# Ten wide matmuls on constants between the sums of squares and unit 0, and ten narrow ones fewer at the start

## What is computed

```python
def rmsnorm(x, g):
    y = x * lax.rsqrt(jnp.mean(x * x, axis=-1, keepdims=True) + EPS)
    return y * g

def ada_norm(x, g, shift, scale):
    return rmsnorm(x, g) * (1 + scale) + shift

for l in range(DEPTH):
    mod = (c @ w_ada[l] + b_ada[l]).reshape(B, N_SUB, 3, D_MODEL)[:, :, :, None, :]
    h = ada_norm(x, norm_gain[l, 0], mod[:, 0, 0], mod[:, 0, 1])
    x = x + 0.5 * mod[:, 0, 2] * swiglu(h, w_ffn_in[l, 0], w_ffn_out[l, 0])
    ...                     # the mixer with mod[:, 1], then the second feed-forward with mod[:, 2]
```

## Time and profile before

| | |
|---|---|
| Median of 3 runs | 1437.67 us (1437.45 to 1437.7) |
| The profiled execution's own time | 1436.94 us |
| Its span, first to last instruction | 1435.1 us |
| TensorE matmuls | 1420.1 us busy, 99% of the span |
| Chain that ended last | PE 91%, DVE 4%, issue 2%, ACT 1%, DMA 1% |
| Granted TensorE clock, mean | 0.998 |

### The profile page before, as it was taken

One profiled execution on the slowest core, in us unless ns is written; L12 is line 12 of the kernel. 1 busy time (PEld: TensorE's weight loads), 2 busy tenths in 40 slices (PEclk: granted clock), 3 DMA queues, 4 the chain that ended last, 5 costly groups with the idle time before them and its releaser, 6 DMA issues.

```text
span 1435.1 us, 33152 instructions
## 1 busy us (share of the span) xinstructions
PE 1420.1 (99%) x13908; PEld 1361.8 (95%) x13908; DVE 949.5 (66%) x1651; ACT 812.1 (57%) x1350; POOL 98.9 (7%) x154
## 2 busy tenths in 40 slices
PE   8999999999999999999999999999999999999998
PEld 6999999999999999999999999999999999999998
DVE  5664547779876697555575545587898677955553
ACT  3554435877676476344464444468876755744543
POOL 3030000001110210000000000000011002000000
PEclk9999999999999999999999999999999999999999
DMA  9988897689984669787768897676999557785661
GB/s 341 308 269 271 243 267 206 177 247 274 245 228 133 198 187 293 217 248 243 202 202 266 273 282 251 198 207 192 261 251 269 165 155 217 225 240 159 178 187 51
DMA packets 460414, 323.75 MB, mean 226 GB/s; under 512 B 11668, under 2 KB 436069, under 8 KB 460266
## 3 DMA queue, kind: packets, MB, share of 16 engines
q1 hardware_dynamic: 452240, 299.96, 71.0%
q0 software_dynamic: 7584, 20.51, 5.2%
q10 hardware_dynamic: 442, 1.17, 0.2%
HBM read 313.29 MB, written 8.37 MB: 224 GB/s over the span
## 4 chain that ended last, share of the span: by engine, by line
PE 91%; DVE 4%; issue 2%; ACT 1%; DMA 1%; ACTq 0%; DVEq 0%
PE bank L513 28%; PE bank L514 27%; PE bank L515 27%; PE bank L704 4%; DVE wlo L478 1%; PE bank L919 1%; DMA stage<-in_x_prompt 1%; PE bank L947 1%; PE bank L966 1%; DVE x L1973 0%; PE bank L988 0%; PE bank L923 0%; PE bank L742 0%; PE bank L1009 0%; ACT xA L1301 0%
## 5 line engine op out<-in xcount | busy, mean ns | idle before, releaser
L478 DVE TENSOR_TENSOR wlo<-raw,whi 128x1024 fp32r<-128x1024 f32 (+1 forms) x432 | 513.1, 1202 | 325.1 <-ACT whi L470 323.8
L513 PE MATMUL bank<-hH,whi 128*128 128x264 f32 x2016 | 578.1, 287 | 0.0
L514 PE MATMUL bank<-hL,whi 128*128 128x264 f32 x2016 | 571.7, 284 | 0.0
L515 PE MATMUL bank<-hH,wlo 128*128 128x264 f32 x2016 | 571.2, 283 | 0.0
L470 ACT ACTIVATE whi<-raw 128x1024 fp32r<-128x1024 f32 (+1 forms) x432 | 438.1, 1033 | 173.5 <-PE bank L515 168.9
L513 PEld LDWEIGHTS bank<-hH,whi 128*128 128x128 f32 x2016 | 379.7, 188 | 13.4 <-issue 12.8
L514 PEld LDWEIGHTS bank<-hL,whi 128*128 128x128 f32 x2016 | 380.0, 189 | 0.0
L515 PEld LDWEIGHTS bank<-hH,wlo 128*128 128x128 f32 x2016 | 378.2, 188 | 0.0
L513 PE MATMUL bank<-hidH,whi 128*128 128x264 f32 x704 | 200.7, 285 | 0.0
L515 PE MATMUL bank<-hidH,wlo 128*128 128x264 f32 x704 | 200.2, 284 | 0.0
L514 PE MATMUL bank<-hidL,whi 128*128 128x264 f32 x704 | 199.6, 284 | 0.0
(11 more groups left out here) (368 smaller groups left out, 1719.4 us busy)
## 6 DMA issues: line engine op xcount, KB each, us to landing
raw<-in_w_ffn_in SPq DMA_DIRECT2D x172, 512.0 KB, 4.8
raw<-in_w_in SPq DMA_DIRECT2D x120, 512.0 KB, 5.3
ring<-in_w_ada SPq DMA_DIRECT2D x96, 512.0 KB, 6.8
raw<-in_w_ffn_out SPq DMA_DIRECT2D x64, 512.0 KB, 4.8
raw<-in_w_ada SPq DMA_DIRECT2D x32, 512.0 KB, 4.1
raw<-in_w_ffn_out SPq DMA_DIRECT2D x32, 384.0 KB, 4.9
raw<-in_w_out SPq DMA_DIRECT2D x16, 512.0 KB, 5.0
out<-st POOLq DMA_DIRECT2D x12, 512.0 KB, 7.7
```

The lines of the kernel that those rows point to most:

```text
L478: nc.vector.tensor_tensor(wlo[:, s, 0:w], raw_unit(n)[:, 0:w], whi[:, s, 0:w].bitcast(F), ALU.subtract).then_inc(lo_done, 1)
L513: nc.tensor.matmul(out, a, rh, start=start, stop=False)
L514: nc.tensor.matmul(out, a, rl, start=False, stop=False)
L515: return nc.tensor.matmul(out, b, rh, start=False, stop=stop)
```

## The change

FILL goes from 43 to 33, and a new constant KEEP is 10. Between the last of the sums of squares and the first feed-forward, ten matmuls are issued on TensorE. Each multiplies 32 columns of the ones tile with its 256 columns, in fp32, into partitions 0 to 31 of the bank AUX[1]. They carry no wait and no semaphore update.

```diff
-FILL = 43
+FILL, KEEP = 33, 10
...
             ada_units(7, 1)
             for k in range(4, KT):
                 add_squares(k)
+            for _ in range(KEEP):
+                mm(AUX[1][0:32, 0:T], ones[:, 0:32], ones[:, :], start=True, stop=True)
             for L in range(NL):
                 ffn(L, 0)
                 mixer(L)
```

## The result

| | before | after |
|---|---|---|
| Median, 22 executions each | 1437.74 us | 1439.61 us |
| Lowest to highest | 1435.60 to 1439.62 | 1437.65 to 1440.89 |
| Ratio, 95% interval | | 1.0012 (1.0006 to 1.0017) |
| Profiled execution, its span | 1436.94, 1435.1 us | 1437.84, 1436.0 us |

The change costs 1.9 us in the median, with an interval of 0.9 to 2.4: slower, but within the 0.2% that the prediction took for no change. The profiled executions differ by 0.9 us.

The account below looks back on a forecast made before the run. TensorE bounds the kernel, with no slack behind the setup. Profiled execution 1436.94 + 0.99 (2.46 us of fillers on the path, unit 0 3.16 instead of 4.63) = 1437.9; against the median, 1438.7 us, range 1436.4 to 1441.8.

Parts of the forecast that it names:

- What bounds the kernel: TensorE, idle only 15.0 of 1435.1 us: whatever moves unit 0 of the first feed-forward moves the end by as much.
- Part 1 costs nothing: Ten small fillers fewer at the start: gain nothing, since line 713 waits for the stage transfer at 12.73 anyway; taken as 0.
- a sign of being wrong: The prediction counted itself wrong if line 713 moved from 12.7 us, fillers started side by side, or the clock fell before 40.
- The price of a wide filler: Between sums of squares and unit 0: twenty records of 0.218 us, 4.36 us; the gap hides 1.9, 2.46 go on the path.
- Does the clock stay high: Wide fillers in the gap before unit 0 hold the clock through 23 to 27 us; chance 0.63, at +0.9 to +1.6 us.
- The first rival: Wide fillers before unit 0 don't hold the clock, or lose it later: +2.6 or +4.4 to +6 us; chance 0.20.
- the rival of overlap: Wide fillers on one column group overlap each other and end inside the gap before unit 0: -1.3 us; chance 0.09.
- small fillers don't lift the clock: Argument against a held clock: start fillers on 32 of 128 columns kept TensorE busy at 4 to 8 us without lifting it.
- What comes back: With the clock held high, unit 0 takes 3.16 us instead of 4.63, ending at 28.61 against 27.62: net +0.99 us.
- The rival that the low stretch comes whatever TensorE does: The clock stays low at 23.1 to 26.5 us regardless, so the fillers run half in it: +2.6 us; chance 0.04.

Follow-up runs that it names:

- part 1 alone: 33 small fillers at the start and no wide ones, against the kernel before: 1445.2 us against 1437.01, ratio 1.0060 (1.0047 to 1.0073).
- 43 + 10: All 43 small fillers kept and ten wide ones added, against the kernel before: 1440.25 us against 1437.01, ratio 1.0020 (1.0011 to 1.0029).
- 38 + 5: 38 small fillers at the start and five wide ones in the gap, against the kernel before: 1436.32 us against 1437.44, ratio 0.9998 (0.9990 to 1.0007).
- 39 + 4: 39 small fillers at the start and four wide ones in the gap, against the kernel before: 1438.09 us against 1437.09, ratio 1.0008 (0.9999 to 1.0016).
- the kernels with the long start: 20 or 21 small and 15 96-column start fillers, three wide behind two modulation units, five or four in the gap, against before: 1435.98 or 1436.03 us.
- five wide: 33 small fillers at the start and five wide ones in the gap, against the kernel before: 1442.47 us, ratio 1.0033 (1.0021 to 1.0046).
- twenty wide: 33 small fillers at the start and twenty wide ones in the gap, against the kernel before: 1443.54 us, ratio 1.0041 (1.0027 to 1.0055).
- 23 + 20: 23 small fillers at the start and twenty wide ones in the gap, against the kernel before: 1444.09 us against 1437.44, ratio 1.0045 (1.0032 to 1.0059).

## Why the prediction was right, and what it mis-sized

**The forecast**, 1438.7 us and no measurable change, holds; the time lies in the range, and the profiled executions differ by 0.9 us where 0.99 was worked out. That this is so close is luck: the end of unit 0 moved by 0.6 and not by 0.99, and 0.2 us of a wait elsewhere and 0.1 unaccounted made up the rest. The median moved by 1.9.

**What bounds the kernel.** Right. What the fillers put in front of unit 0 reached the end: 0.6 us at line 704 behind it, 0.2 us in one wait, and 0.1 us unaccounted.

**Part 1 costs nothing.** Right for the reason given, the wait for the stage tile, and borne out with ten small fillers back in the program (ratio 0.9998, 0.9990 to 1.0007). Line 713 did move, to 12.33, which the prediction had as a sign of being wrong; but it moved with the tile's landing, which puts it anywhere from 12.3 to 13.3 in the traces with the short start, with no order by the number of fillers. The zero is right only because the number of matmuls stayed 43, which the prediction didn't see. Had the change dropped the ten without adding ten, it would have cost the 8 us of part 1 alone, outside the range. No row of before hinted at a size; the wait named issue near its end is 0.5 us.

**The price of a wide filler.** 0.218 us a record predicted, 0.216 measured, in two kernels. The gap hid 1.9 us of it and unit 0 starts 2.06 us later than before; 2.46 was worked out, and 0.3 of the 0.4 between them is that the fillers start at 20.64 and not at 20.93: the stage tile had landed 0.4 us earlier.

**Does the clock stay high.** Yes, through 4.4 us after, and through 8.8 us with twenty. The first rival, fillers that don't hold it, is out. So is the rival of overlap, by the 0.216. But one argument of the step was wrong: that small fillers don't lift the clock. They didn't in the execution that was read. They did in the profiled ones with 43 + 10, 38 + 5 and several others, by 7 to 9 us. The prediction read one execution of a thing that varies from one to the next; 1.07 against 1.93 us for the first two units of line 704 is the sign to look for.

**What comes back, the term that was mis-sized.** 1.47 us in unit 0, counted for every execution. It comes back only where the clock had fallen at 23 us. Of the kernels with nothing wide in the gap, the profiled executions of part 1 alone and of ten small ones in the gap have no fall there (unit 0 is over at 26.59 and 26.76); that with the ten moved behind the first mixer has it (28.41, from a start at 23.78). Counted from the end of the sums, unit 0 is over 6.5 and 6.7 us later where the clock falls (before, and the ten moved), 5.3 and 5.4 where it doesn't, and 7.4 in all three traces with ten wide fillers. So the fillers cost 0.7 to 0.9 us where the clock would have fallen, and 2.0 to 2.1 where it wouldn't. A mixture of these fits the 1.9 of the median, but it is argued, not shown: how many executions of before are of which kind can't be counted from their mean clocks. The view prints 0.998 for the execution before, with the fall at 23, for 39 + 4, whose fall is at 12, and for the kernels with the long start, which have none before the end. Nor does it say why both groups moved by at least 1.5.

**The rival that the low stretch comes whatever TensorE does.** Its price was 2.6 us; the profiled execution after has no fall at 23 us, and the ten executions at 0.999 have no room for one (at most 2.2 us are missing, where a fall like that of before and the one at the end make 2.9). But it had a point: with 1.90 and 2.02 us idle the clock fell in two traces, with 1.86 us it didn't in another. The page named beside it (the Trainium skill, TensorE: Matmul & The Clock Gate, "What's actually happening") says that the same kernel finds its point of change in another place from run to run. The traces agree. Six of the kernels are the same on TensorE up to the gap, 33 small fillers and what follows them, and the clock first rises at 16.3 (part 1 alone), 15.3 (after), 7.6 (five wide), 7.1 (twenty wide), 6.9 (ten small) and 7.4 (the ten moved). The prediction had that to weigh and took one place for all.

## What to carry to other kernels

When filler or any other instruction is added or dropped, keep the number on the engine the same and move it, or the experiment can measure standstills elsewhere in the program instead: here 5 to 8 us with five or ten matmuls fewer, against 0 to 2 for the fillers themselves, and nothing that can be told with ten more. Look at the middle of the trace for waits named issue between two instructions that wait for nothing. A gain that rests on the clock's state in one profiled execution should be multiplied by the share of executions in which that state occurs; make the state sure first (here with 6.4 us of fillers at the start and three more in the wait behind them), then count.

## What the runs showed of the hardware

- With ten matmuls fewer in front TensorE stood still for 2.9 and 3.5 us shortly behind a burst of 128 records of small matmuls, at 358 and at 1061 us; with the ten put back anywhere ahead of the burst that standstill was gone.
- When the clock first rose, at 6.9 to 8.8 us in eight traces, TensorE had done nothing but fillers on 32 of the array's 128 columns since 3.6 us, and small transposes in some. In four others (before, after, part 1 alone, 23 + 20) it rose only at 15.3 to 17.1 us. In both traces with 6.4 us of fillers it rose at 9.2.
- Once fallen, the clock can stay low through work that is dense by the busy row: with 43 + 10 it was at 0.50 from 12.2 to 22.4 us, over the transposes and most of line 704.
- A matmul of 256 fp32 columns on one column group costs 0.43 us at the high clock, the same as four of them side by side on four groups.
